# Four gate tiles among block one's first convolution tiles, with buffers of their own for gates and mixer outputs

## Chip, core and metric

The kernel runs on one core of one Trainium2 chip. The metric is the device time of one execution in microseconds. PE is TensorE (PEld its weight loads), DVE VectorE, ACT ScalarE, POOL GpSimd, SP SyncE, which issues the weight DMAs.

## The reference, cut to what matters

Two blocks run one after the other over 256 tokens of width 1024, all in float32. Block one is a Mamba-2 mixer and a gated linear recurrence side by side, and the change lies inside it:

```
hn = rmsnorm(h, norm1_w);  proj = hn @ w_in
gates, z, xbc, dt_raw, lru_x, lru_y = split(proj)
gates = sigmoid(gates + b_branch_gate)
xbc = silu(causal_dwconv(xbc));  dt = softplus(dt_raw + dt_bias)
y = ssd_chunked(xs * dt, dt * a, B, C) + xs * d_skip        # xs, B, C are cut from xbc
y_ssm = rmsnorm_per_group(y * silu(z)) @ w_out_ssm
u = causal_dwconv(lru_x)
r, i = sigmoid(u @ w_r + b_r), sigmoid(u @ w_i + b_i)       # ten heads of 128
log_a = -8 * r * softplus(-lam);  a = exp(log_a)
h_t = a * h_(t-1) + sqrt(1 - a^2) * (i * u)                  # a scan over the tokens
y_lru = (h_t * gelu(lru_y)) @ w_out_lru
h = h + (g_ssm * y_ssm + g_lru * y_lru) @ w_out
```

A feed-forward part follows, and then block two (attention branches and feed-forward, twice), which the change does not touch.

## The kernel before

All weights pass through in 256-column (or 256-row) tiles of 1 MB, in the order of `tile_names()`. For each tile SP loads a raw slot (three of them), ACT copies it to `w_hi` in fp32r, DVE (POOL for a share of later ones) subtracts to get `w_lo`, and PE multiplies: per product the three parts hi*hi, hi*lo, lo*hi, so 16 products or 48 matmuls of 256 columns for a tile. The results stand in PSUM (a ring of four banks, "low", for the tiles; another of four, "high", for small stages).

All engines walk the same list of tiles (`walk`). At tile i each of ACT and DVE does, in this order: `lead(i)`, the split of tile i + 2, which needs PE to have finished tile i - 1; `rest` of tile i - 1; the "mid" stages that `stage_order()` puts at tile i; `evac` of tile i, which needs PE to have finished tile i. PE does the mid stages of a tile halfway through its matmuls (`columns`), and from there its queue is in order: a stage that waits holds the second half of the tile and all that follows.

Tiles of block one before: dt; lx 0 to 4; bc 0 to 3; xs 0, xs 1; then (xs 2+j, ly j, gate j) for j = 0 to 4; xs 7; gate 5 to 7; z and out_ssm tiles. What they cost beside the split:

- `lx`, `bc`, `xs`: ACT opens a convolution (`conv_open`, two instructions), DVE does six steps (`conv`). For bc and xs the rest is a Tanh on ACT and one product on DVE, which ticks `xbc`.
- `gate`: ACT alone, two Tanh of 256 columns. The gates lie over `lru_ab`, the recurrence's a and b, so a gate tile waits for its scans (`lru_scan`).
- `ly`: one Square and one Tanh on ACT, three steps on DVE.

Stages: `gates_ready` (the softplus of dt and lambda: a chain that goes between DVE and ACT, with three ACT table loads), `lru` h (one head: eight short matmuls for two heads, five ACT instructions, two on DVE; it needs the `lam` that gates_ready ends with), `dt_cs` (a cumulative sum on DVE; ACT then issues a DMA that waits for it), `lru_root` (a Sqrt on ACT between two table loads), `lru_scan`, and the SSD: `ssd_open` g (PE: products of B and C and eight transposes of xs), `ssd_decay`, `ssd_val`. `ssd_open` g begins on PE with

```
pe.wait_ge(*at("xbc", 6 + 2 * g))
```

that is for the product of xs tile 2g + 1, since four bc tiles count too. The 21 SSD steps stand one to a tile, in order, from the tile that `places` begins with; the steps with `ssd_open` are steps 0, 5, 10 and 15.

Of the kernel before, what the change touches and what calls it, by code (L numbers as in the profile page):

```python
# [7 lines left out]
F32 = mybir.dt.float32  # L8
# [5 lines left out]
P = 128  # L14
SEQ = 256
# [74 lines left out]

def tile_names():
    names = [("dt", 0)]
    names += [("lx", j) for j in range(5)]
    names += [("bc", j) for j in range(4)]
    names += [("xs", 0), ("xs", 1)]
    for j in range(5):
        names += [("xs", 2 + j), ("ly", j), ("gate", j)]
    names += [("xs", 7)] + [("gate", j) for j in range(5, 8)]
    for g in range(GROUPS):
        names += [("z", 2 * g), ("z", 2 * g + 1)]  # L100
        if g >= 2:
# [85 lines left out]
def stage_order():  # L187
    order = {}

    def put(where, tile, *stages):  # L190
        order.setdefault((where, T[tile]), []).extend(stages)

    put("mid", ("lx", 2), ("gates_ready",))
    for tile, heads in ((("lx", 3), (0, 1)), (("lx", 4), (2, 3))):
        put("mid", tile, *[("lru", h) for h in heads])
    put("mid", ("bc", 0), ("lru", 4), ("lru", 5))
    put("mid", ("bc", 1), ("dt_cs",), ("lru", 6), ("lru", 7))
    put("mid", ("bc", 2), ("lru", 8))
    put("mid", ("bc", 3), ("dt_turn",), ("lru", 9))
    put("mid", ("xs", 0), ("lru_root", 0))  # L200
    put("mid", ("xs", 1), ("lru_root", 1))
    for j in range(5):
        put("mid", ("xs", 2 + j), ("lru_scan", 2 * j), ("lru_scan", 2 * j + 1))

    ssd = []
    for g in range(GROUPS):
# [1 line left out]
        for p in range(4):  # L208
            ssd.append(([("ssd_val", g, p - 1)] if p else []) + [("ssd_decay", g, p)])
    ssd.append([("ssd_val", GROUPS - 1, 3)])  # L210
    places = TILES[T["xs", 3]:T["z", 4] + 1]
    assert len(places) == len(ssd)
    for tile, stages in zip(places, ssd):
        put("mid", tile, *stages)
# [97 lines left out]
def build(nc, w, x_t, x_tok, rows_w, params, consts, consts_2, out_tok):  # L312
    ctx = ExitStack()
    with ctx:
        def sb(name, shape, dt=F32, stack=ctx):
            return stack.enter_context(nc.sbuf_tensor(name, shape, dt))
# [45 lines left out]
        one = ExitStack()  # L362
        xbc = sb("xbc", [P, XBC // P, SEQ], stack=one)
        lru_u = sb("lru_u", [P, LC, SEQ], stack=one)
        lru_ab = sb("lru_ab", [P, 2 * LC, SEQ], stack=one)
        lru_a, lru_b, gates = lru_ab[:, 0:LC, :], lru_ab[:, LC:2 * LC, :], lru_ab[:, 0:2 * DC, :]
        cs_all = sb("cs_all", [P, HPG, SEQ], stack=one)
        xdt = sb("xdt", [P, TT, GC * P], stack=one)
        z_silu = sb("z_silu", [P, 2 * GC, SEQ], stack=one)
# [62 lines left out]
        def pair(x):  # L432
            return x.rearrange("p (k t) -> p k t", k=2)
# [79 lines left out]
        def pe_program():  # L513
# [205 lines left out]
            def rows_ready(name, j):  # L719
                if name == "out_ssm":  # L720
                    pe.wait_ge(*at("y_hi", j + 1))
                    pe.wait_ge(*at("y_lo", j + 1))
                    return 8 + GC * (j // 2 % 2) + 2 * (j % 2)
                if name == "out_lru":
                    pe.wait_ge(*at("lru_hi", j + 1))
                    pe.wait_ge(*at("lru_lo", j + 1))
                    return 2 * j
                if name == "out":
                    pe.wait_ge(*at("mix_hi", j + 1))
                    pe.wait_ge(*at("mix_lo", j + 1))  # L730
                    return 2 * j
                if name in ("ffn_out", "down"):
                    n = j + 1 + (NF1 if name == "down" else 0)
                    pe.wait_ge(*at("h_hi", n))
                    pe.wait_ge(*at("h_lo", n))
                    return 2 * ((j % NF2 if name == "down" else j) % 4)
                l, j = divmod(j, 4)
                if j == 0:
                    pe.wait_ge(*at("ret_hi", 2 * l + 2))
                    pe.wait_ge(*at("ret_lo", 2 * l + 2))  # L740
                else:
                    a = {1: "dsa", 2: "dil0", 3: "dil1"}[j]
                    pe.wait_ge(*at(f"{a}_hi", 2 * l + 2))
                    pe.wait_ge(*at(f"{a}_lo", 2 * l + 2))
                return 2 * j

            def rows(i, name, j):
                count, ring = ROWS[name]
                whole, n = divmod(OUT_ORDER.index(j % 4) + 4 * (j // 4) if name == "out_2" else j, count)
                first, last = n == 0, n == count - 1  # L750
                hi, lo = tile_ready(i)
                k0 = rows_ready(name, j)
                if name not in ("out_ssm", "out_lru"):
                    return token_rows(i, name, j, whole, first, last, ring, hi, lo, k0)
                for b in range(DC // 2):
                    if first:
                        acc[name, b] = take(ring, (name, whole, b), freed_acc(name, whole, b))
                    bank = acc[name, b]
                    for j2 in range(2):
                        for m in range(2):  # L760
                            c0 = (2 * b + m) * P
                            inst = product(bank[:, m * SEQ:(m + 1) * SEQ], hi[:, j2, c0:c0 + P], lo[:, j2, c0:c0 + P],
                                           act_hi[:, k0 + j2, :], act_lo[:, k0 + j2, :], first and j2 == 0 and m == 0,
                                           last and j2 == 1)
                    if last and b < DC // 2 - 1:
                        inst.then_inc(*tick("acc_done"))
                inst.then_inc(*tick("tile_used"))
# [236 lines left out]
        def act_program():  # L1004
# [24 lines left out]
            def evac(i, name, j):  # L1029
# [12 lines left out]
                    k0 = 2 * j + (16 if name == "bc" else 0)  # L1042
                    conv_open(xbc[:, k0:k0 + 2, :], bank, "conv_w", XBC // P, "conv_b", k0, "xbc_open")
                if name == "gate":
                    act.wait_ge(*at("lru_scan", 2 * (j % 5) + 2))
                    act.wait_ge(*at("halved", 3))
                    for m in range(2):
                        inst = fn(gates[:, 2 * j + m, :], bank[:, m * SEQ:(m + 1) * SEQ], ACT.Tanh, scale=0.5,
                                  bias=param("b_gate", 2 * j + m))
                    inst.then_inc(*tick("gate"))  # L1050
# [129 lines left out]

            def norm_split(g):
                for s in range(2):
                    k = 8 + GC * (g % 2) + 2 * s
                    act.wait_ge(*at("gn_x", 2 * g + s + 1))
                    if g >= 2:
                        act.wait_ge(*used("out_ssm", 2 * (g - 2) + s))
                    fn(act_hi[:, k:k + 2, :], pair(tmp[8 + s][:, :]), ACT.Copy).then_inc(*tick("y_hi"))

            def lru_split(n):
                act.wait_ge(*at("lru_out", n + 1))  # L1190
                act.wait_ge(*(used("out_ssm", 4) if n == 4 else used("z", 7)))
                fn(act_hi[:, 2 * n:2 * n + 2, :], lru_u[:, 2 * n:2 * n + 2, :], ACT.Copy).then_inc(*tick("lru_hi"))

            def mix():
                for b in range(4):
# [798 lines left out]
        def pool_program():  # L1994
            def tt(out, a, b, op):
                return nc.gpsimd.tensor_tensor(out, a, b, op)  # L1996

            def low_part(k, n, src):
                return tt(act_lo[:, k:k + n, :], src, act_hi[:, k:k + n, :].bitcast(F32), ALU.subtract)

            split = {"next": 0}

# [22 lines left out]
            def norm_split(g):  # L2025
                for s in range(2):
                    pool.wait_ge(*at("y_hi", 2 * g + s + 1))
                    low_part(8 + GC * (g % 2) + 2 * s, 2, pair(tmp[8 + s][:, :])).then_inc(*tick("y_lo"))

            def lru_split(n):  # L2030
                pool.wait_ge(*at("lru_hi", n + 1))
                low_part(2 * n, 2, lru_u[:, 2 * n:2 * n + 2, :]).then_inc(*tick("lru_lo"))

            pool.wait_ge(*at("x1_hi", 3))
            low_part(4, 2, pair(tmp[8][:, :])).then_inc(*tick("x1_lo_pool"))
# [93 lines left out]
```

## Time and profile before

| | |
|---|---|
| median of 3 runs | 1224.14 us (1223.98 to 1224.82) |
| the profiled execution | 1226.08 us, its span 1224.8 us |
| mean granted clock | 0.993 |
| PE busy | 1185.3 us (97%) |
| DVE busy | 804.1 us (66%) |
| ACT busy | 700.0 us (57%) |
| HBM | 171 GB/s over the span |

An engine's busy time is the union of its instructions. A PE that is busy has work in flight. Of the chain that ended last 79% is PE's. Times below are microseconds from the start of the span.

### The profile page before, as it was taken

The page shows a single profiled execution, that of the slowest core. Times are in us where ns is not written, and L with a number is a line of the kernel's source. Part 1 is how long each engine was busy: PE and PEld are TensorE (multiplying, and loading weights), DVE is VectorE, ACT ScalarE, POOL GpSimd, SP SyncE. Part 2 cuts the span into 40 slices and gives each one's busy share as a digit, 9 for nine tenths or more (in the row PEclk, how much of TensorE's full clock was granted, in tenths as well). Part 3 has the DMA queues.
Part 4 walks back from the last instruction along what each step waited for, and adds up shares of the span by engine and source line. Part 5 has one row for each costly group of instructions (what it writes and reads, how often), then busy time and mean ns, then how long its engine had stood idle before and what let it go on. Part 6 is the DMA issues. An engine that isn't in the chain of part 4 may idle for free.

```text
span 1224.8 us, 18917 instructions
## 1 busy us (share of the span) xinstructions
PE 1185.3 (97%) x7688; PEld 1057.1 (86%) x7688; DVE 804.1 (66%) x1044; ACT 700.0 (57%) x964; POOL 322.6 (26%) x207
## 2 busy tenths in 40 slices
PE   9798999999999999999999899999999989999997
PEld 9798999999998888888999688888899977888886
DVE  7878988677456766675878555555556963555554
ACT  6788766676435443435646856444554396555543
POOL 0000000034931111111475522122225654222211
PEclk9899999999999999999999999999999999999999
DMA  9434756544456665554643346665554433565560
GB/s 291 164 123 154 241 173 202 178 138 142 177 199 238 207 201 176 196 182 139 194 134 122 104 141 207 202 199 181 162 184 147 162 104 104 174 229 185 185 207 34
DMA packets 152437, 210.66 MB, mean 172 GB/s; under 512 B 5504, under 2 KB 132640, under 8 KB 151712
## 3 DMA queue, kind: packets, MB, share of 16 engines
q1 hardware_dynamic: 151584, 205.08, 51.5%
q10 hardware_dynamic: 768, 4.39, 0.9%
q8 instruction: 61, 1.00, 0.3%
q14 instruction: 24, 0.20, 0.0%
HBM read 208.37 MB, written 1.08 MB: 171 GB/s over the span
## 4 chain that ended last, share of the span: by engine, by line
PE 79%; ACT 10%; DVE 8%; issue 2%; DMA 1%; POOL 0%; SPq 0%; ACTq 0%; DVEq 0%
PE banks L534 77%; ACT w_hi L1008 2%; ACT tmp L1008 2%; DVE w_lo L1398 2%; ACT L1008 2%; PE banks L542 1%; DVE xbc L1406 1%; ACT probs_dil L1008 1%; DMA raw<-in_w_in 1%; DVE work L1402 1%; ACT lru_ab L1008 1%; ACT probs_dsa L1008 0%; ACT xbc L1008 0%; DVE lru_u L1406 0%; DVE tmp L1406 0%
## 5 line engine op out<-in xcount | busy, mean ns | idle before, releaser
L534 PE MATMUL banks<-act,w_hi 128*128 128x256 f32 (+1 forms) x3216 | 732.0, 317 | 16.0 <-DVE w_lo L1398 12.0
L534 PEld LDWEIGHTS banks<-act,w_hi 128*128 128x128 f32 x3216 | 524.1, 191 | 65.0 <-issue 19.9
L534 PE MATMUL banks<-act,w_lo 128*128 128x256 f32 (+1 forms) x2040 | 562.2, 282 | 0.0
L1398 DVE TENSOR_TENSOR w_lo<-raw,w_hi 128x2048 fp32r<-128x2048 f32 (+4 forms) x174 | 366.5, 2108 | 222.3 <-ACT w_hi L1008 221.6
L1008 ACT ACTIVATE w_hi<-raw 128x2048 fp32r<-128x2048 f32 (+1 forms) x191 | 359.6, 1884 | 188.6 <-PE banks L534 180.6
L534 PEld LDWEIGHTS banks<-act,w_lo 128*128 128x128 f32 (+1 forms) x2040 | 382.7, 191 | 1.4
L534 PE MATMUL banks<-w_hi,act 128*128 128x512 f32 (+1 forms) x1072 | 323.1, 376 | 7.1 <-DVE act L1398 6.5
L1996 POOL TENSOR_TENSOR w_lo<-raw,w_hi 128x512 fp32r<-128x512 f32 (+1 forms) x146 | 202.6, 1416 | 432.7 <-ACT w_hi L1008 432.7
L534 PEld LDWEIGHTS banks<-w_hi,act 128*128 128x128 f32 x1072 | 197.3, 190 | 46.7 <-issue 11.0
L1996 POOL TENSOR_TENSOR act<-tmp,act 128x512 fp32r<-128x512 f32 x52 | 112.6, 2169 | 451.6 <-ACT act L1008 451.6
L534 PE MATMUL banks<-w_lo,act 128*128 128x512 f32 (+1 forms) x536 | 200.1, 373 | 0.0
L1008 ACT ACTIVATE tmp<-tmp 128x512 f32<-128x512 f32 (+1 forms) x112 | 64.7, 592 | 140.9 <-DVE tmp L1409 140.3
L534 PEld LDWEIGHTS banks<-w_lo,act 128*128 128x128 f32 x536 | 101.8, 190 | 16.1 <-issue 0.5
L1409 DVE TENSOR_REDUCE tmp<-banks 128x512 f32<-128x1024 f32 x54 | 66.0, 1222 | 48.2 <-PE banks L534 48.2
L1008 ACT ACTIVATE act<-tmp 128x512 fp32r<-128x512 f32 x55 | 34.9, 635 | 24.7 <-DVE tmp L1406 22.2
L1008 ACT ACT_TABLE_LOAD x29 | 37.2, 1283 | 1.7 <-PEq L2122 1.2
L1406 DVE SCALAR_TENSOR_TENSOR xbc<-banks,params,xbc 128x255 f32<-128x255 f32 (+2 forms) x72 | 29.1, 474 | 5.9 <-ACT xbc L1008 5.9
L1008 ACT ACTIVATE probs_dil<-probs_dil,small 128x128 f32<-128x128 f32 x64 | 26.2, 451 | 4.8 <-DVE small L1885 2.7
L1008 ACT ACTIVATE tmp<-cs_all,cs_tok 128x256 f32<-128x256 f32 x64 | 23.7, 445 | 0.0
L1406 DVE SCALAR_TENSOR_TENSOR act<-banks,params,act 128x256 fp32r<-128x256 f32 x32 | 13.3, 478 | 15.6 <-ACT act L1008 15.6
L1008 ACT ACTIVATE tmp<-residual 128x512 f32<-128x512 f32 x23 | 14.3, 641 | 9.2 <-DVE residual L1406 9.2
L1398 DVE TENSOR_TENSOR act<-banks,act 128x256 fp32r<-128x256 f32 x12 | 5.0, 419 | 22.1 <-ACT act L1008 21.9
(228 smaller groups left out, 739.7 us busy)
## 6 DMA issues: line engine op xcount, KB each, us to landing
raw<-in_w_in SPq DMA_DIRECT2D x64, 1024.0 KB, 5.3
raw<-in_w_up SPq DMA_DIRECT2D x32, 1024.0 KB, 5.3
raw<-in_w_down SPq DMA_DIRECT2D x32, 1024.0 KB, 5.0
raw<-in_w_ffn_in SPq DMA_DIRECT2D x22, 1024.0 KB, 5.1
raw<-in_w_out SPq DMA_DIRECT2D x12, 1024.0 KB, 5.0
raw<-in_w_ffn_out SPq DMA_DIRECT2D x11, 1024.0 KB, 4.9
raw<-in_w_out_ssm SPq DMA_DIRECT2D x8, 1024.0 KB, 4.9
raw<-in_w_out_lru SPq DMA_DIRECT2D x5, 1024.0 KB, 4.9
```

The lines of the kernel that those rows point to most:

```text
L534: return mm_ops.matmul(out, lhs, rhs, start=start, stop=stop, skip_group_check=True)
L542: return mm_ops.transpose(out, a, c["ident"][0:k, 0:k])
L1008: return ops.activation(out, a, func, bias=bias, scale=scale, accum_out=accum)
L1398: return ops.tensor_tensor(out, a, b, op)
L1402: return ops.tensor_scalar(out, a, s1, None, op0)
L1406: return ops.scalar_tensor_tensor(out=out, in0=a, scalar=s, in1=b, op0=op0, op1=op1, accum_out=accum)
L1409: return ops.tensor_reduce(pair(out[:, :]), both.rearrange("p m (a t) -> p m t a", a=2), AX_X, ALU.add)
L1996: return nc.gpsimd.tensor_tensor(out, a, b, op)
```

## The change

The tiles of block one come in another order: dt; lx 0, 1, 2; gate 0; lx 3; gate 1; lx 4; bc 0; gate 2; bc 1; bc 2; gate 3; bc 3; xs 0, xs 1; then (xs 2+j, gate 4+j, ly j) for j = 0 to 3; xs 6; ly 4; xs 7; then z as before. The softplus (`gates_ready`) goes from lx 2 to gate 0, the ten heads from lx 3 to bc 3 to five tiles from gate 1 to gate 3, `dt_cs` from bc 1 to bc 2, `dt_turn` from bc 3 to xs 0, the scans from the xs tiles to the gate tiles and ly 4. The 21 SSD steps begin at xs 2 and end at z 5, where they began at xs 3 and ended at z 4. The gates get the upper half of `act` (free since the third tile), and the mixer's outputs, which lay there, get `late`, which lies over `lru_ab`; the waits that guarded the old overlays go or are replaced. The bytes, matmuls and vector instructions are the same in number.

```diff
     names = [("dt", 0)]
-    names += [("lx", j) for j in range(5)]
-    names += [("bc", j) for j in range(4)]
-    names += [("xs", 0), ("xs", 1)]
-    for j in range(5):
-        names += [("xs", 2 + j), ("ly", j), ("gate", j)]
-    names += [("xs", 7)] + [("gate", j) for j in range(5, 8)]
+    names += [("lx", 0), ("lx", 1), ("lx", 2), ("gate", 0), ("lx", 3), ("gate", 1), ("lx", 4), ("bc", 0), ("gate", 2), ("bc", 1),
+              ("bc", 2), ("gate", 3), ("bc", 3), ("xs", 0), ("xs", 1)]
+    for j in range(4):
+        names += [("xs", 2 + j), ("gate", 4 + j), ("ly", j)]
+    names += [("xs", 6), ("ly", 4), ("xs", 7)]
...
-    put("mid", ("lx", 2), ("gates_ready",))
-    for tile, heads in ((("lx", 3), (0, 1)), (("lx", 4), (2, 3))):
+    put("mid", ("gate", 0), ("gates_ready",))
+    for tile, heads in ((("gate", 1), (0, 1, 2, 3)), (("bc", 0), (4,)), (("gate", 2), (5, 6, 7)), (("bc", 1), (8,)),
+                        (("gate", 3), (9,))):
         put("mid", tile, *[("lru", h) for h in heads])
-    put("mid", ("bc", 0), ("lru", 4), ("lru", 5))
-    put("mid", ("bc", 1), ("dt_cs",), ("lru", 6), ("lru", 7))
-    put("mid", ("bc", 2), ("lru", 8))
-    put("mid", ("bc", 3), ("dt_turn",), ("lru", 9))
-    put("mid", ("xs", 0), ("lru_root", 0))
+    put("mid", ("bc", 2), ("dt_cs",))
+    put("mid", ("xs", 0), ("dt_turn",), ("lru_root", 0))
     put("mid", ("xs", 1), ("lru_root", 1))
     for j in range(5):
-        put("mid", ("xs", 2 + j), ("lru_scan", 2 * j), ("lru_scan", 2 * j + 1))
+        put("mid", ("gate", 4 + j) if j < 4 else ("ly", 4), ("lru_scan", 2 * j), ("lru_scan", 2 * j + 1))
...
-    places = TILES[T["xs", 3]:T["z", 4] + 1]
+    places = TILES[T["xs", 2]:T["z", 5] + 1]
...
+        with ExitStack() as shared:
+            sb("act_first", [P, 8, 2, SEQ], F32R, stack=shared)
+            gates = sb("gates", [P, 2 * DC, SEQ], stack=shared)
         both_parts = sb("act", [P, 16, 2, SEQ], F32R)
...
-        lru_ab = sb("lru_ab", [P, 2 * LC, SEQ], stack=one)
-        lru_a, lru_b, gates = lru_ab[:, 0:LC, :], lru_ab[:, LC:2 * LC, :], lru_ab[:, 0:2 * DC, :]
+        with ExitStack() as shared:
+            lru_ab = sb("lru_ab", [P, 2 * LC, SEQ], stack=shared)
+        late = sb("late", [P, 2 * LC, SEQ], F32R, stack=one)
...
                 if name == "gate":
-                    act.wait_ge(*at("lru_scan", 2 * (j % 5) + 2))
                     act.wait_ge(*at("halved", 3))
...
             def norm_split(g):
                 for s in range(2):
-                    k = 8 + GC * (g % 2) + 2 * s
+                    k = GC * (g % 2) + 2 * s
+                    act.wait_ge(*at("lru_scan", LC))
...
-                fn(act_hi[:, k:k + 2, :], pair(tmp[8 + s][:, :]), ACT.Copy).then_inc(*tick("y_hi"))
+                fn(y_hi[:, k:k + 2, :], pair(tmp[8 + s][:, :]), ACT.Copy).then_inc(*tick("y_hi"))
...
-                act.wait_ge(*(used("out_ssm", 4) if n == 4 else used("z", 7)))
-                fn(act_hi[:, 2 * n:2 * n + 2, :], lru_u[:, 2 * n:2 * n + 2, :], ACT.Copy).then_inc(*tick("lru_hi"))
+                act.wait_ge(*(at("lru_scan", LC) if n == 4 else used("z", 7)))
+                fn(last_hi if n == 4 else act_hi[:, 2 * n:2 * n + 2, :], lru_u[:, 2 * n:2 * n + 2, :], ACT.Copy).then_inc(*tick("lru_hi"))
```

The same replacement of `act_hi`/`act_lo` by the views of `late` stands in PE's `rows` and in POOL's `low_part`.

## Rows read from the trace of the kernel before

**Rows 1.** Busy time by stretch of time: us, then each engine, granted clock, DMA share.
```profile
33.00:49.70 16.70, 15.45 (x112) 14.65 (x112) 12.78 (x30) 10.66 (x16) 0.00 (x0) 1.00 0.56 179
49.70:55.50 5.80, 0.00 (x0) 0.00 (x0) 5.70 (x14) 5.59 (x11) 0.00 (x0) 0.87 0.00 0
55.50:61.00 5.50, 5.46 (x25) 5.48 (x26) 5.50 (x11) 5.43 (x11) 0.00 (x0) 0.52 0.61 194
61.00:95.00 34.00, 31.81 (x244) 30.64 (x242) 26.40 (x49) 27.38 (x48) 0.00 (x0) 1.00 0.40 126
95.00:122.70 27.70, 23.98 (x193) 23.31 (x193) 23.94 (x41) 23.48 (x26) 0.00 (x0) 1.00 0.50 152
122.70:211.00 88.30, 87.74 (x727) 83.68 (x728) 78.69 (x112) 61.45 (x105) 0.00 (x0) 1.00 0.63 203
211.00:234.00 23.00, 23.00 (x193) 21.64 (x192) 15.05 (x22) 13.47 (x23) 0.00 (x0) 1.00 0.63 212
```

**Rows 2.** Waits of PE from 33 to 130 us: total, times, longest.
```profile
PE banks L534 <- DVE w_lo L1398: 11.8, 7, 5.9
```

**Rows 3.** PE in order of time: start, duration, instruction, count, idle before it.
```profile
55.54 0.77 PE L534 MATMUL banks<-act,w_hi 128*128 128x256 f32 x2 [5.87 <-DVE w_lo L1398]
...
122.66 0.47 PE L534 MATMUL banks<-act,w_hi 128*128 128x256 f32 x2 [1.25 <-DVE w_lo L1398]
...
125.12 0.28 PE L534 MATMUL banks<-act,w_lo 128*128 128x256 f32 x1
...
125.48 0.28 PE L534 MATMUL banks<-act,w_lo 128*128 128x256 f32 x1
125.60 0.82 PE L534 MATMUL banks<-xbc 128*128 128x256 f32 x4
...
152.85 0.88 PE L534 MATMUL banks<-tmp,xdt 128*64 128x256 f32 x8
153.66 0.50 PE L534 MATMUL banks<-act,w_hi 128*128 128x256 f32 x2
```

**Rows 4.** ACT in order of time from softplus to the heads, same columns.
```profile
44.47 0.42 ACT L1008 ACTIVATE cs_all<-cs_all 32x256 f32<-32x256 f32 x1 [2.21 <-DVE small L1398]
...
47.62 1.90 ACT L1008 ACTIVATE w_hi<-raw 128x2048 fp32r<-128x2048 f32 x1
49.53 1.28 ACT L1008 ACT_TABLE_LOAD   x1
...
78.16 0.84 ACT L1008 ACTIVATE tmp<-banks,params 128x256 f32<-128x256 f32 x2 [3.84 <-DVE cs L1591]
...
80.48 0.82 ACT L1008 ACTIVATE tmp<-banks,params 128x256 f32<-128x256 f32 x2
```

**Rows 5.** ACT in order of time around the second root, same columns.
```profile
108.38 1.27 ACT L1008 ACTIVATE lru_ab<-lru_ab 128x1280 f32<-128x1280 f32 x1
109.55 1.00 ACT L1008 ACTIVATE xbc<-banks,params 128x256 f32<-128x256 f32 x2
110.45 1.91 ACT L1008 ACTIVATE w_hi<-raw 128x2048 fp32r<-128x2048 f32 x1
112.38 1.28 ACT L1008 ACT_TABLE_LOAD   x1
113.67 0.63 ACT L1008 ACTIVATE tmp<-xbc 128x512 f32<-128x512 f32 x1
```

**Rows 6.** DVE in order of time: last step of softplus, then tile xs 1.
```profile
50.67 0.17 DVE L1402 TENSOR_SCALAR small<-small 128x10 f32<-128x10 f32 x1
...
110.66 2.43 DVE L1406 SCALAR_TENSOR_TENSOR xbc<-banks,params,xbc 128x255 f32<-128x255 f32 x6 [2.01 <-ACT xbc L1008]
113.00 2.28 DVE L1398 TENSOR_TENSOR w_lo<-raw,w_hi 128x2048 fp32r<-128x2048 f32 x1
115.20 0.68 DVE L1406 SCALAR_TENSOR_TENSOR xbc<-tmp,xbc 128x512 f32<-128x512 f32 x1
```

**Rows 7.** ACT and DVE in order of time after PE has finished tile xs 4.
```profile
150.09 1.02 ACT L1008 ACTIVATE xbc<-banks,params 128x256 f32<-128x256 f32 x2 [1.90 <-PE banks L534]
...
151.72 2.42 DVE L1406 SCALAR_TENSOR_TENSOR xbc<-banks,params,xbc 128x255 f32<-128x255 f32 x6
154.06 2.28 DVE L1398 TENSOR_TENSOR w_lo<-raw,w_hi 128x2048 fp32r<-128x2048 f32 x1
...
156.25 0.68 DVE L1406 SCALAR_TENSOR_TENSOR xbc<-tmp,xbc 128x512 f32<-128x512 f32 x1
```

More of the change, by code:

```diff
@@ L364, in build @@
         lru_u = sb("lru_u", [P, LC, SEQ], stack=one)
-        lru_ab = sb("lru_ab", [P, 2 * LC, SEQ], stack=one)
-        lru_a, lru_b, gates = lru_ab[:, 0:LC, :], lru_ab[:, LC:2 * LC, :], lru_ab[:, 0:2 * DC, :]
+        with ExitStack() as shared:
+            lru_ab = sb("lru_ab", [P, 2 * LC, SEQ], stack=shared)
+        late = sb("late", [P, 2 * LC, SEQ], F32R, stack=one)
+        lru_a, lru_b = lru_ab[:, 0:LC, :], lru_ab[:, LC:2 * LC, :]
+        y_hi, y_lo, last_hi, last_lo = late[:, 0:8, :], late[:, 8:16, :], late[:, 16:18, :], late[:, 18:20, :]
         cs_all = sb("cs_all", [P, HPG, SEQ], stack=one)
@@ L722, in rows_ready @@
                     pe.wait_ge(*at("y_lo", j + 1))
-                    return 8 + GC * (j // 2 % 2) + 2 * (j % 2)
+                    return GC * (j // 2 % 2) + 2 * (j % 2)
                 if name == "out_lru":
@@ L754, in rows @@
                     return token_rows(i, name, j, whole, first, last, ring, hi, lo, k0)
+                x_hi, x_lo = (y_hi, y_lo) if name == "out_ssm" else (act_hi, act_lo)
+                if (name, j) == ("out_lru", 4):
+                    x_hi, x_lo, k0 = last_hi, last_lo, 0
                 for b in range(DC // 2):
@@ L762, in rows @@
                             inst = product(bank[:, m * SEQ:(m + 1) * SEQ], hi[:, j2, c0:c0 + P], lo[:, j2, c0:c0 + P],
-                                           act_hi[:, k0 + j2, :], act_lo[:, k0 + j2, :], first and j2 == 0 and m == 0,
+                                           x_hi[:, k0 + j2, :], x_lo[:, k0 + j2, :], first and j2 == 0 and m == 0,
                                            last and j2 == 1)
@@ L1996, in tt, with low_part @@
                 return nc.gpsimd.tensor_tensor(out, a, b, op)
-            def low_part(k, n, src):
-                return tt(act_lo[:, k:k + n, :], src, act_hi[:, k:k + n, :].bitcast(F32), ALU.subtract)
+            def low_part(k, n, src, hi=act_hi, lo=act_lo):
+                return tt(lo[:, k:k + n, :], src, hi[:, k:k + n, :].bitcast(F32), ALU.subtract)
             split = {"next": 0}
@@ L2027, in norm_split @@
                     pool.wait_ge(*at("y_hi", 2 * g + s + 1))
-                    low_part(8 + GC * (g % 2) + 2 * s, 2, pair(tmp[8 + s][:, :])).then_inc(*tick("y_lo"))
+                    low_part(GC * (g % 2) + 2 * s, 2, pair(tmp[8 + s][:, :]), y_hi, y_lo).then_inc(*tick("y_lo"))
             def lru_split(n):
                 pool.wait_ge(*at("lru_hi", n + 1))
-                low_part(2 * n, 2, lru_u[:, 2 * n:2 * n + 2, :]).then_inc(*tick("lru_lo"))
+                src = lru_u[:, 2 * n:2 * n + 2, :]
+                (low_part(0, 2, src, last_hi, last_lo) if n == 4 else low_part(2 * n, 2, src)).then_inc(*tick("lru_lo"))
             pool.wait_ge(*at("x1_hi", 3))
```

## The prediction, made before the changed kernel was run

> **What bounds the kernel now.** I read the page first: PE is busy in 97% of the span and most of the chain that ended last is PE's, so an edit counts only where it changes PE's idle time or its clock. The busy times by stretch say where that is in block one [rows 1]. PE has nothing in flight from 49.7 to 55.5, its clock is at 0.52 from 55.5 to 61, and it loses 2.2 of 34 us and 3.7 of 27.7 us in the two stretches up to 122.7. From there to 211 it loses 0.6 of 88.3 and then none. The waits name DVE's `w_lo` [rows 2]. It is late because ACT and DVE are full there: softplus and ten heads stand on top of the convolutions. In the stretch 211 to 234, with three of the gate tiles, DVE has 8 of 23 us free. The change carries four gate tiles, which cost DVE only their split, to the place where PE starves.
>
> One tile of PE is 5.76 us: three matmuls (one product) take 0.36, from 125.12 to 125.48 [rows 3], and a tile has 16 products. Without any wait tiles lx 3 to gate 0 (11 tiles, 63.4 us), ten heads (0.86 each, a tile with two heads being 1.72 longer) and 0.5 for `dt_turn` would take 72.5 us. They take from 33.05 to 122.66 [rows 3], so 89.6, and 17.1 us is lost. That is the most the front can give back: 5.87 of it in one gap [rows 3], and 5.5 x (1 - 0.52) = 2.6 by the clock behind it [rows 1].
>
> **Part 1, the front.** I wrote the queues of PE, ACT and DVE side by side, each instruction in program order, beginning when its engine is free and its wait is met. From start to start ACT pays 1.80 for a split, 0.90 for opening a convolution and 0.54 for a Tanh of 512 [rows 5, 7], 2.32 for a head (78.16 to 80.48), 1.30 for a table load [rows 4], 1.17 for a root [rows 5]; DVE 2.34 for a convolution, 2.20 for a split, 0.60 for the product that ticks `xbc` [rows 6]. Done for the kernel before, the table puts xs 3 at 121.7 (trace 122.66) and the losses of 33 to 275 us at 17.6 where the trace has 18.5 (the 17.1 and 1.3 behind it), so it is 0.9 short; I charge the changed kernel with the same 0.9.
>
> For the new order it gives these marks. PE does gate 0 from 33.05 to 39.0, waits 1.9 for lx 3's `w_hi`, and 1.7 for gate 1's `w_lo` (48.2), because DVE has two splits and a convolution to do. Softplus now comes behind gate 1's split on DVE; it ends at 55.2 where it ended at 50.8 [rows 6], and lx 4's split stands behind it, ready at 57.4, just as PE ends gate 1 at 57.6 with four heads in it. So the 5.87 gap is gone, and the clock stays up. Four heads on ACT end at 67.3; behind them stand gate 1's Tanh and gate 2's split, and PE waits 2.4 (69.9 to 72.3). After that it waits only 0.5 at xs 0. The front loses 6.5 in place of 17.1, and PE begins xs 2 at 117.9.
>
> **Part 2, where it goes.** At xs 2 PE meets `ssd_open` 0 halfway, at 120.8, and this waits for the sixth `xbc`: the product of xs 1, the tile just before. In the old order a whole tile lay between (xs 2), and the product, at 115.20 + 0.68 = 115.9 [rows 6], was 9.7 us early for the 125.60 of [rows 3]. So it must be read from ACT when it comes now. From the fourth head's end (67.3) to the second root's end ACT has nine splits (16.2), six heads (13.9), six openings (5.4), five Tanh of 512 (2.7), three gate Tanh (0.71 each, 2.1), two roots (2.3), three table loads (3.9) and the DMA's issue (0.45), 47.0 in all. To this come waits for DVE, of which the table has 9.5: the convolution before each Tanh, and `dt_cs`, where ACT stands still until the sum is there (the 3.84 in [rows 4]). That makes 123.8. Then as in [rows 5, 6]: opening, convolution to 127.2, DVE's split and the product, done at 130.0. PE waits 9.3. The 9.5 is the softest term; the same stretch before has 7.0 (the 3.84 and four of 0.77 to 0.78), and I put its ends at 7 and 12, the wait at 6.8 to 11.8. The front's gain is real, but ACT's and DVE's work ahead of this point has not shrunk, and the wait hands it back.
>
> **Part 3, the same wait twice more.** `ssd_open` 2 is step 10 and now stands at gate 7, right behind xs 5; `ssd_open` 3 is step 15, at z 0, right behind xs 7. `ssd_open` 1 (ly 1) has a tile between and is free. After PE has finished xs 4 (ACT starts at 150.09) the product is there at 156.25 + 0.68 = 156.9 [rows 7], 6.9 later, of which DVE was behind by 0.6. PE arrives half a tile (2.9) and one `ssd_val` (0.8 to 1.0, [rows 3]) later, so 3.8 to 3.9. The difference is 2.4 to 3.1 each; the table has 2.7 and 2.8. Both stand on the path: PE is the bound there [rows 1], and the next splits are ready by 7 us, so nothing else would have held it. Nothing hides them, as the second half of the tile is queued behind.
>
> **Part 4, the clock.** The wait of 9.3 at xs 2 is longer than the 5.87 in which the clock fell. There the half clock cost 2.6 after work had resumed [rows 1]. I take 2.6 again; the ends are 0 (it falls and is back up early) and 5.2 (twice that). The granted clock was 0.52 in the stretch behind that gap, which is the 1.2 GHz level. The Trainium skill says (TensorE: Matmul & The Clock Gate, "What's actually happening") that the throttled state is the default and that activity releases it; by that rule too this change, which looks like one that feeds PE more evenly, pays for a half clock at xs 2. The trace agrees, by that 0.52.
>
> **Part 5, what costs nothing.** The gates' old wait for the scans goes: no engine waited for it, as the scans were done tiles before. `norm_split` gets a wait for the tenth scan, done at ly 4, six tiles before. The fifth LRU split loses its wait for out_ssm 4, but stays queued behind out_ssm 5's stages. The new buffers move no data. The residual's DMA goes two tiles later in SP's queue; the DMA share is 0.4 to 0.6 there [rows 1], its 1 MB and the raw tile behind it have 10 us, and the residual is not read before block one's end. `lru_scan` and `ssd_decay` come closer together at the end: xs 6, ly 4 and xs 7 give DVE about 7.3 each (a split 2.2, a convolution 2.34, the ly steps or scans 2, the SSD's 1.4), against 6.75 for PE, so DVE falls 1.5 behind over three tiles, under the 7 us of lead. Small waits of PE on `ssd_m` and on the norm's total sum to 2.9 in the table, against the 1.3 of before.
>
> **The sum.** After: 1.9 + 1.7 + 2.4 + 0.5 in front, 9.3, 2.7, 2.8, small ones 2.9, clock 2.6, the table's 0.9: 27.7. Before: 18.5. The change costs 9.2 us. Against the profiled execution, 1226.08 of device time, that is 1235.3; it lies 1.9 over the median, so I say 1224.14 + 9.2 = 1233.3. Behind z 5 all is as before and PE-bound, so I see nothing that would take it up.
>
> **Rivals.**
> A, the clock holds or costs little: +6.6, 1230.7. For it: it fell only once in block one. Against: the wait is the longer one.
> B, the other side: the product of xs 1 is ready when PE arrives. If ACT's waits for DVE vanish in the front (9.5 to 0), the product is there at 120.5 and `ssd_open` 0 costs nothing; the sum is then 9.2 - 9.3 - 2.6, that is -2.7, or 1221.4. It decides at 120.8. For it: gates relieve DVE. Against: the convolution must precede its Tanh, and ACT has this pair on its own path each time (the 2.01 of [rows 6] and 3.84 of [rows 4]). With half of that, 4.6 less wait and no clock fall, the sum is +2: within the noise.
> C, DVE goes over its lead behind xs 6 and splits come late, or two falls of the clock: another 3 to 6, 1236 to 1239. For it: 7.3 against 6.75, with steps 13 to 19 beside. Against: PE's own waits at gate 7 and z 0 give DVE time.
> D, table loads cost more than the row shows. A load takes 1.28 (112.38) and the Tanh starts at 113.67 [rows 5], 0.01 later. The Trainium skill (ScalarE: Activation LUTs, "What ACT_TABLE_LOAD costs") gives 2.66 us with a drain. By that page's figure the four loads ahead of the sixth product would add an estimated 4 x 1.38 = 5.5 to the wait, 1239. The row decides against it; its chance lies within C's.
>
> **Chances.** Forecast, 1231.5 to 1235.5: 0.50. A: 0.15. C with D: 0.17. B: 0.08 in full, 0.10 at the half, of which I count most as no change. Faster by over 0.2% (2.4 us, about what a measurement of this kernel can tell from none) 0.09, within it 0.09, slower 0.82. The range leaves out B in full and half of C: 1225 to 1238.
>
> **What would show it.** In the changed trace: no gap near 50 us, clock 1.0 up to 120; PE with about 9 us idle, ended by DVE's `xbc`, at about 121, before `banks<-xbc`; two more of 2 to 3 us near 205 and 243; a low clock only behind the first. Wrong would be: a wait at xs 2 under 5 us, or waits for `w_lo` in the place of those for `xbc`.

## The result, and the profile after

The changed kernel takes 1238.03 us (median of 4 runs, 1237.62 to 1242.12) against 1224.48 for the kernel before (4 runs on the same chip, 1223.98 to 1226.52). The ratio is 1.0114 with a 95% interval of 1.0103 to 1.0126: 13.5 us slower. I had said 1233.3, in a range of 1225 to 1238. The sign and the place were right; the size was 4.7 us short, and the time lies just outside the range.

| | before | changed |
|---|---|---|
| the profiled execution, its span | 1226.08, 1224.8 us | 1237.99, 1236.7 us |
| mean granted clock | 0.993 | 0.989 |
| PE busy | 1185.3 us (97%) | 1188.0 us (96%) |
| DVE, ACT busy | 804.1, 700.0 us | 806.3, 700.2 us |
| tile z 6 begins on PE | 287.29 | 300.84 |

All of it is lost ahead of z 6, 13.55 us by the last line. (The two spans differ by 11.9, because the profiled execution of before lost 1.6 more in one wait at 1008 us, which the change doesn't touch.)

Waits of PE from 33 to 300 us in the changed kernel: what it waited for, then us in total, times, longest. Line 537 is the matmul helper, 534 in the kernel before.

```profile
PE banks L537 <- DVE xbc L1412: 14.5, 3, 8.6
PE banks L537 <- DVE tmp L1404: 3.8, 4, 3.0
PE banks L537 <- DVE w_lo L1404: 3.8, 2, 2.3
PE banks L537 <- ACT w_hi L1014: 1.8, 1, 1.8
```

Of the 11.8 for `w_lo` of [rows 2] 3.8 is left, and the gap of 5.87 of [rows 3] is gone. Three waits for `xbc`, none of which was there before, cost 14.5. That is what I had described. What I hadn't is in the second line: 3.8 for `tmp`, of which 2.97 is one wait for the norm at z 5. Here are PE's instructions at which three of the four long waits end, start and duration first, the idle time ahead and its releaser last:

```profile
131.00 1.41 PE L537 MATMUL banks<-xbc 128*128 128x256 f32 x3 [8.60 <-DVE xbc L1412]
...
205.83 0.88 PE L537 MATMUL banks<-xbc 128*128 128x256 f32 x2 [2.87 <-DVE xbc L1412]
...
283.32 1.13 PE L537 MATMUL banks<-tmp,mean_group 128*128 128x256 f32 x4 [2.97 <-DVE tmp L1404]
```

The fourth is 3.06 at z 0 (242.10 to 245.15). Busy time by stretch, as in [rows 1] (length, PE, PEld, DVE, ACT, POOL, granted clock, DMA share, GB/s):

```profile
33.00:48.20 15.20, 11.93 (x97) 11.58 (x97) 12.87 (x24) 8.18 (x10) 0.00 (x0) 1.00 0.71 239
70.00:76.50 6.50, 4.17 (x23) 3.99 (x22) 6.30 (x8) 6.43 (x12) 0.00 (x0) 0.74 0.40 126
76.50:122.40 45.90, 45.90 (x366) 45.00 (x365) 35.77 (x59) 35.87 (x53) 0.00 (x0) 1.00 0.53 167
122.40:131.00 8.60, 0.01 (x1) 0.03 (x1) 6.44 (x10) 6.82 (x7) 0.00 (x0) 0.81 0.62 196
131.00:134.50 3.50, 3.50 (x14) 3.32 (x15) 1.38 (x3) 0.00 (x0) 0.00 (x0) 0.50 1.00 365
202.90:210.00 7.10, 4.23 (x22) 4.08 (x21) 6.86 (x10) 0.63 (x1) 0.00 (x0) 0.76 0.62 200
237.00:250.00 13.00, 9.95 (x84) 9.42 (x84) 10.12 (x18) 4.51 (x8) 0.00 (x0) 1.00 0.73 243
280.00:289.00 9.00, 6.03 (x37) 5.68 (x34) 5.36 (x6) 7.29 (x10) 6.17 (x4) 0.81 0.12 40
```

The third line is the front's gain: 45.9 us in which PE doesn't stop once, where before it lost something in nearly every tile. The clock column tells the rest. It is low behind four gaps, of 2.33, 8.6, 2.87 and 2.97 us, and stays at 1.00 behind the one of 3.06 (seventh line). In the fifth line it is 0.50, the 1.2 GHz level, over 3.5 us of work: 1.75 us lost. Elsewhere it is (1 - 0.74) x 6.5 = 1.7, (1 - 0.76) x 7.1 = 1.7 and (1 - 0.81) x 9.0 = 1.7, each with the low stretch wholly in work. Together 6.9 us, against the 2.6 of [rows 1] before.

### The profile page after: what moved, and what is told of

The parts are those of the page before. It is cut to its first block, busy times and chain, and to the rows that moved or that the text cites. A ratio compares the mean times of both kernels' runs of the same rounds, so it can differ in the third digit from the quotient of the medians.

```text
span 1236.7 us, 18911 instructions
## 1 busy us (share of the span) xinstructions
PE 1188.0 (96%) x7688; PEld 1060.0 (86%) x7688; DVE 806.3 (65%) x1044; ACT 700.2 (57%) x964; POOL 322.9 (26%) x207
## 4 chain that ended last, share of the span: by engine, by line
PE 74%; DVE 12%; ACT 10%; issue 3%; DMA 1%; POOL 0%; SPq 0%; ACTq 0%; DVEq 0%
PE banks L537 72%; ACT w_hi L1014 2%; DVE xbc L1412 2%; DVE w_lo L1404 2%; ACT tmp L1014 2%; PE banks L545 2%; ACT L1014 1%; ACT probs_dil L1014 1%; DVE lru_u L1412 1%; DMA raw<-in_w_in 1%; DVE tmp L1404 1%; DVE work L1408 1%; ACT xbc L1014 1%; DVE tmp L1412 0%; ACT probs_dsa L1014 0%
## 5 line engine op out<-in xcount | busy, mean ns | idle before, releaser
L537 PE MATMUL banks<-act,w_hi 128*128 128x256 f32 (+1 forms) x2928 | 680.5, 320 | 10.4 <-DVE w_lo L1404 4.0
L537 PEld LDWEIGHTS banks<-act,w_hi 128*128 128x128 f32 x2928 | 480.4, 191 | 58.7 <-issue 13.1
L537 PE MATMUL banks<-act,w_lo 128*128 128x256 f32 x1896 | 522.0, 282 | 0.0
L537 PEld LDWEIGHTS banks<-act,w_lo 128*128 128x128 f32 x1896 | 355.7, 191 | 1.4
L2002 POOL TENSOR_TENSOR act<-tmp,act 128x512 fp32r<-128x512 f32 x44 | 102.4, 2327 | 440.1 <-ACT act L1014 440.1
L537 PE MATMUL banks<-late,w_hi 128*128 128x256 f32 x288 | 52.2, 284 | 0.0
L537 PEld LDWEIGHTS banks<-late,w_hi 128*128 128x128 f32 x288 | 45.0, 192 | 0.1
L537 PE MATMUL banks<-late,w_lo 128*128 128x256 f32 x144 | 40.7, 283 | 0.0
L1014 ACT ACTIVATE act<-tmp 128x512 fp32r<-128x512 f32 x47 | 29.9, 635 | 4.6 <-DVE tmp L1412 2.1
L537 PEld LDWEIGHTS banks<-late,w_lo 128*128 128x128 f32 x144 | 27.6, 192 | 0.0
```

The source lines that it names most:

```text
L537: return mm_ops.matmul(out, lhs, rhs, start=start, stop=stop, skip_group_check=True)
L1014: return ops.activation(out, a, func, bias=bias, scale=scale, accum_out=accum)
```

## The experiments

Two theories stood after the result. Mine: three `ssd_open` stand a tile too close behind the `xs` tile whose product they read; these waits, the norm's and the clock behind them are the whole loss. The rival: something else that comes with the change, the buffers or the new neighbours on ACT and DVE, has moved the loss, and `xbc` is only where it shows. Each run is timed beside the kernel before, whose median stands with it where it matters. The traces and pages quoted are of one profiled execution each.

One number of the prediction has to be set right first. It says that in the old order a whole tile lay between xs 1 and `ssd_open` 0. By the list of tiles it was three: xs 2, ly 0 and gate 0, as the stage stood in the middle of xs 3. `ssd_open` 2 and 3 had three and two tiles between them and the xs tile that they read. The change put each of the three stages straight behind it, with none between.

### The three openings one tile later

```diff
+    for g in (0, 2, 3):
+        ssd[5 * g].remove(("ssd_open", g))
+        ssd[5 * g + 1].insert(0, ("ssd_open", g))
```

> The changed kernel with ssd_open 0, 2 and 3 each one tile later (gate 4, ly 3, z 1), so that a whole tile lies between an xs tile and the stage that reads it. Theory (PE waits for the product of the xs tile just before it): the waits of 8.6, 2.9 and 3.1 us go, and with them the clock falls at 127.7 and 206.2 that cost about 1.7 each; 1238.0 - 14.6 - 3.4 gives 1220.0, between 1218 and 1222, faster than the kernel before. Rival (the front has gained nothing, DVE and ACT are behind anyway, and PE then waits for w_lo or the SSD's masks instead): 1228 or more, with new waits of 5 us or more between 120 and 260.

Measured: 1225.12 (1222.72 to 1226.10), ratio 0.9996 (0.9987 to 1.0006). One tile more, for three openings of one stage, gives back 13 us, and the changed kernel stands where the kernel before does. Its waits of PE from 33 to 300:

```profile
PE banks L540 <- DVE xbc L1415: 2.9, 1, 2.9
...
PE banks L540 <- DVE tmp L1407: 3.8, 4, 3.0
```

```profile
130.67 1.22 PE L540 MATMUL banks<-xbc 128*128 128x256 f32 x3 [2.87 <-DVE xbc L1415]
```

The waits at `ssd_open` 2 and 3 are gone. That at `ssd_open` 0 isn't: PE reaches it at 127.80, a tile later, and the product of xs 1 still ends at 130.5. I had expected no wait here. The time lies 5 us over the forecast, of which this wait and the low clock behind it (130.9 to 134.3) are 4.6, and the reason is on view: the product comes no earlier, and a tile's 5.8 us isn't enough for a lag of 8.6. One tile between is less than the three of the kernel before. The norm's 2.98 is untouched.

### The first opening alone

The same edit with `for g in (0,)`.

> Only ssd_open 0 one tile later (gate 4). Theory: 8.6 of wait and 1.7 of half clock go: 1227.7, the waits at gate 7 and z 0 stay at 2.9 and 3.1. Rival (PE, ahead again, finds the later products later by as much): the waits at gate 7 and z 0 grow by some us each, 1231 to 1235.

Measured: 1233.31 (1230.96 to 1235.54), ratio 1.0068 (1.0050 to 1.0086). That is 4.7 of the change's loss. Waits at the three openings are now 3.85, 2.87 and 3.05 and at the norm 2.97. So the 8.6 shrank to 3.85 by 4.75, and the later two stayed as they were: each is its own wait, not an echo of the first. Against the run above, openings 2 and 3 are worth another 8.2: their waits sum to 5.9, and the 2.3 left are put down to the clock, which was low behind both of them here (1.7 and 2.9 us lost in the profiled execution, the slowest of the four) and behind neither there. (The wait at opening 0 is 1.0 shorter there because PE came 0.9 later, its clock having fallen at 73; it ends at the same time, 130.7, in both.) In this kernel's profile the clock was low behind each of the four waits, for 3.4 us behind the first two and 6.8 us behind the last two.

### The buffers alone

The kernel before, with its own order of tiles and stages, and the new buffers (`gates` in `act_first`, mixer outputs in `late`, with their waits).

```diff
-        lru_ab = sb("lru_ab", [P, 2 * LC, SEQ], stack=one)
+        with ExitStack() as shared:
+            lru_ab = sb("lru_ab", [P, 2 * LC, SEQ], stack=shared)
+        late = sb("late", [P, 2 * LC, SEQ], F32R, stack=one)
...
-                    act.wait_ge(*at("lru_scan", 2 * (j % 5) + 2))
```

> The order of tiles and stages of the kernel before, with the changed kernel's buffers and waits only. Theory (buffers cost and give nothing): within 1 us of the kernel before, 1224.5. Rival (the new buffers are part of the loss, by reads of late on PE or by the wait for the tenth scan): 1227 or more.

Measured: 1225.10 (1223.96 to 1225.91), ratio 1.0002 (0.9992 to 1.0011), with the waits of before:

```profile
PE banks L540 <- DVE w_lo L1407: 11.9, 7, 5.9
```

The rival loses its first half: places and waits of the buffers cost nothing.

### The kernel before with an early opening

```diff
+    ssd[0].remove(("ssd_open", 0))
+    put("mid", ("xs", 2), ("ssd_open", 0))
```

> The kernel before with ssd_open 0 alone one xs tile earlier, at xs 2, straight behind xs 1. Theory: PE arrives at 104.4 and waits for the product at 115.9, so 11.5 us; the waits for w_lo of 0.7, 1.3 and 1.3 behind it go, ly 1 starts 7.7 later than at 130.0, and a clock fall adds 1.7 to 2.6: 1224.5 + 9.4 to 10.3, so 1234 to 1235. Rival (the wait only takes the place of waits that PE has anyway, since ACT and DVE are the bound there): 1224 to 1227.

Measured: 1234.39 (1232.86 to 1235.38), ratio 1.0074 (1.0058 to 1.0091).

```profile
115.40 1.41 PE L536 MATMUL banks<-xbc 128*128 128x256 f32 x3 [11.43 <-DVE xbc L1408]
```

A stage moved from the middle of xs 3 to the middle of xs 2, three tiles earlier in the old order, costs 9.6 us between the medians, 9.1 by the ratio: the wait of 11.43, plus 2.6 for a half clock that lasts 5.2 us into the work behind it, less 3.2, three of the four waits for `w_lo` from 101 to 123 (among those of [rows 2]), which vanish while PE stands. That is 10.8; the stretch after it (tile ly 1) begins 9.6 us later than before in an execution that had begun 0.6 earlier, so 10.2. So taking the tiles away between a product and its reader is enough for such a loss, without any gate tile.

### The norm's wait

At z 4 DVE does `norm_split` 0 ahead of the last two mask products, which become a stage of their own.

```diff
-    put("mid", ("z", 4), ("norm_split", 0), ("norm_sum", 1))
+    put("mid", ("z", 4), ("norm_split", 0), ("last_mask",), ("norm_sum", 1))
```

> The changed kernel with one thing turned round on DVE at z 4: the first group's norm (reciprocal and two scalings) stands ahead of the last two mask products, which z 4 did not have in the old order. Theory (those products, 2.6 us beside POOL's split, push the norm's total late): PE's wait for the mean at z 5 falls from 2.97 to under 1.2, and with it the clock fall at 284.7 (1.7): 1238.0 - 1.9 - 1.7, so 1234.4, between 1233 and 1236.5. Rival (the wait comes from the outputs' new buffer): no change, 1237 to 1239.

Measured: 1234.92 (1233.48 to 1238.76), ratio 1.0086 (1.0070 to 1.0103). DVE's instructions there from the split on, of the changed kernel and then of this one (a convolution step of 0.48 is left out behind each split):

```profile
272.47 1.23 DVE L1404 TENSOR_TENSOR w_lo<-raw,w_hi 128x1024 fp32r<-128x1024 f32 x1 [0.32 <-ACT w_hi L1014]
...
274.27 2.57 DVE L1404 TENSOR_TENSOR tmp<-tmp,cb_mask 128x384 f32<-128x384 f32 x2
276.76 1.74 DVE L1653 RECIPROCAL rstd<-rstd 128x256 f32<-128x256 f32 x1
278.53 1.67 DVE L1412 SCALAR_TENSOR_TENSOR tmp<-z_silu,params,rstd 128x256 f32<-128x256 f32 x4
```

```profile
275.81 1.22 DVE L1404 TENSOR_TENSOR w_lo<-raw,w_hi 128x1024 fp32r<-128x1024 f32 x1 [0.31 <-ACT w_hi L1014]
...
277.39 1.75 DVE L1655 RECIPROCAL rstd<-rstd 128x256 f32<-128x256 f32 x1
279.17 1.74 DVE L1412 SCALAR_TENSOR_TENSOR tmp<-z_silu,params,rstd 128x256 f32<-128x256 f32 x4
280.83 1.01 DVE L1404 TENSOR_TENSOR tmp<-tmp,cb_mask 128x384 f32<-128x384 f32 x2
```

```profile
PE banks L537 <- DVE tmp L1404: 0.8, 3, 0.3
```

In the changed kernel the mask products hold the reciprocal back by 2.5. Done later they take 1.01, and the norm's wait of 2.97 is no longer among PE's waits. That is worth 3.1 us between the medians; I had expected 3.6. The profiled execution is the slowest of the four (1238.76): the clock didn't fall behind the norm, but it did at z 0, and was low for 6.8 us there. Of the 3.1 us, how much is the wait and how much the clock isn't shown.

### PE kept at work through the waits

34 products of a constant with itself (`mm`, two matmul records each) ahead of the wait of `ssd_open` 0 and 10 ahead of those of 2 and 3, into a bank that the stage then begins anew. They add no work to another engine and are to end before the wait does; only the clock should differ.

```diff
+                for _ in range({0: 34, 2: 10, 3: 10}.get(g, 0)):
+                    mm(bank[:, 0:P], c["mean_d"], c["mean_d"])
```

> The changed kernel with matmuls on a constant put in front of the three waits for xbc (34, 10 and 10 calls, 7.7, 2.3 and 2.3 us of PE at full clock), into the bank that the stage then overwrites. The waits themselves stay. Theory (half clock behind the waits costs 1.7 at xs 2 and 1.6 at gate 7): these two falls go and the time is 1238.0 - 3.3, so 1234.7, between 1233.5 and 1236. Rival (the clock costs nothing on the path): 1238 or more.

Measured: 1236.17 (1234.62 to 1236.46), ratio 1.0087 (1.0072 to 1.0103). 1.9 gained where I expected 3.3. The 34 calls were too few: PE still stood 1.91 at xs 2, and the clock fell there and behind the norm; behind gate 7's it didn't. So it was done again with 39, 12 and 12, and 12 ahead of the norm's mean:

> The changed kernel with all four long waits of PE filled by matmuls on a constant: 39 calls ahead of the wait at xs 2 (8.8 us), 12 each at gate 7, z 0 and ahead of the norm's mean at z 5 (2.7 us each). The waits stay. Theory (the term of the sum that was too small is the clock, three falls of 1.6 to 1.7 us behind these waits): no half clock between 100 and 400 us, and 1238.0 - 5 + 0.5 for the calls' ends gives 1233.5, between 1232 and 1235. Rival (the falls take nothing from the path): 1237 or more.

Measured: 1233.89 (1233.18 to 1234.41), ratio 1.0071 (1.0057 to 1.0085). One stretch, 100 to 300 us:

```profile
100.00:300.00 200.00, 197.00 (x1625) 188.40 (x1624) 158.99 (x223) 138.54 (x209) 13.12 (x9) 1.00 0.50 164
```

The same stretch of the changed kernel has a clock of 0.97. Here it is 1.00, the profile has no low clock ahead of 689 us, and z 6 begins at 296.36 and not at 300.84. The wait at xs 2 ends at 131.33, no earlier than in the changed kernel (this execution began 0.4 later), though PE came to it 1.0 earlier by the same start: the low clock at 73 had been taken up by that wait. So of the 13.5 us the clock has about 4, by 1238.03 - 1233.89, and some 9 that remain are waits. Between the two profiled executions, from the same start, z 6 comes 4.9 earlier.

### Both mended

Later openings with the norm's order on DVE:

> Both repairs on the changed kernel: ssd_open 0, 2 and 3 one tile later, and the first norm ahead of the last mask products on DVE. Theory: 2 to 3.5 us under the kernel with the later opens alone (1225.1): 1221.6 to 1223.1, faster than the kernel before by 0.1 to 0.25%. Rival (what is won falls to other waits): 1225.

Measured: 1221.46 (1220.01 to 1223.46) against 1224.91, ratio 0.9971 (0.9959 to 0.9982). Then ACT's DMA for `cs`, which waits for DVE's sum, goes from bc 2 to bc 3:

```diff
+    put("mid", ("bc", 3), ("cs_spill",))
```

> The same, and ACT issues the DMA of the cumulative sums one tile later (bc 3 in place of bc 2), so that it does not stand 3.8 us for DVE. Theory (ACT's queue up to the second root sets when the sixth xbc product comes): the product comes 2 to 3.8 us earlier, PE's remaining wait of 2.9 at gate 4 goes to under 1 and its clock fall with it: 1218.5 to 1221.5. Rival (DVE, not ACT, sets it): the product stays at about 130.6 and the time at that of the kernel without this.

Measured: 1220.73 (1218.34 to 1221.39), ratio 0.9960 (0.9948 to 0.9973). This is the fastest of all: the change of order is worth 0.4% once its readers stand a tile further from their products and the norm goes first on DVE. The last edit gave less than I expected of it:

```profile
PE banks L541 <- DVE xbc L1416: 2.7, 1, 2.7
```

The product that PE waits for is read 2.5 earlier (128.31 in place of 130.79, of which 0.8 is an earlier start of the whole execution), and the wait stays at 2.7 because PE, too, arrives earlier: in this profile its clock didn't fall at 73, nor at 42. Between the last two medians the intervals overlap; the DMA's place is not shown to matter.

### The first opening still later

The kernel just described, with `ssd_open` 0 and the masks that read it behind gate 4's matmuls instead of in its middle.

> The best kernel so far (later opens, norm ahead, the sums' DMA later; 1220.7) with ssd_open 0 and the first decay behind gate 4's matmuls in place of between them. Theory: PE comes there 2.9 us later, its last wait for xbc of 2.7 us and the fall behind it go, less up to 2 of wait for the first masks at ly 0: 1217 to 1219.5. Rival (the masks come so much later that PE waits for them instead): 1220.5 to 1222.

Measured: 1220.67 (1220.35 to 1221.35), ratio 0.9964 (0.9952 to 0.9977): no change, as the rival had it.

```profile
PE banks L544 <- DVE tmp L1411: 4.6, 4, 3.8
```

The wait for `xbc` is gone, and one of 3.76 for the first masks stands in its place, ahead of `ssd_val`. The chain from the sixth product over the masks to the values has its own length, and PE met it here at the next reader.

### The softplus back at its old place

The changed kernel, with `gates_ready` at lx 2.

```diff
-    put("mid", ("gate", 0), ("gates_ready",))
+    put("mid", ("lx", 2), ("gates_ready",))
```

> The changed kernel with softplus back at lx 2, ahead of the splits of gate 1 and lx 4 on both queues. Theory (what the front wins the wait at xs 2 takes back, since ACT's and DVE's queues set when the sixth xbc product comes): PE waits some 7 us more before gate 1 (w_lo at about 55.4 in place of 48.0), and 6 to 8 us less at xs 2 (8.6 to 1 or 2), so the time stays at 1238 within 2 us. Rival (the front's waits and the wait at xs 2 add up): 1243 to 1246.

Measured: 1244.57 (1241.34 to 1246.08), ratio 1.0153 (1.0134 to 1.0171). The time is the rival's; its reason is only a part of it.

```profile
PE banks L537 <- DVE xbc L1412: 12.9, 3, 7.0
PE banks L537 <- DVE w_lo L1404: 7.2, 1, 7.2
```

With softplus early DVE brings gate 1's split late, and PE stands 7.2 there (48.36 to 55.54). My theory was that this is taken from the 8.6 at xs 2, as the sixth product's time was set by ACT and DVE alone. But ACT's first head needs PE's matmuls, which stand in gate 1 behind the same wait:

```profile
61.25 0.84 ACT L1014 ACTIVATE tmp<-banks,params 128x256 f32<-128x256 f32 x2 [5.08 <-PE banks L537]
```

So ACT loses 5.08 as well, the product comes at 133.9 in place of 130.9, and the wait at xs 2 falls only from 8.6 to 7.0. PE's waits for `w_lo` and `xbc` together are yet only 1.8 longer than in the changed kernel (7.2 and 12.9 against 3.8 and 14.5). Most of the rest is the clock. In the profiled execution it was low for longer behind the waits at z 0 and of the norm, here with their stretches:

```profile
247.00:254.00 7.00, 5.62 (x24) 5.47 (x25) 3.57 (x6) 0.00 (x0) 0.00 (x0) 0.51 0.49 160
288.00:295.00 7.00, 5.85 (x23) 5.48 (x24) 4.99 (x5) 5.07 (x5) 4.21 (x3) 0.51 0.08 6
```

That is 2.8 and 2.9 us lost in work, where the changed kernel lost nothing and 1.7; behind the three openings and the norm it sums to 9.3 against 5.2. With the 3.1 by which the wait at xs 2 ends later this makes 7.2, and z 6 begins 7.0 later. It is the change's move of softplus that spares the front the gap of 7.2.

## Why the prediction came out as it did

**Part 1, the front: right in its waits, wrong in its clock.** Forecast 6.5 of waits; measured 1.83 for lx 3's `w_hi`, 1.44 and 2.33 for `w_lo`, none at xs 0: 5.6. PE began xs 2 at 119.37 where I had 117.9. The waits were 0.9 shorter than forecast, and PE still came 1.5 later. 1.7 of these 2.4 are the low clock from 73.0 to 76.5, behind the 2.33 us gap, in a place where I had written "the clock stays up"; the other 0.7 are of the size of the 0.9 that I had added for what the table misses.

**Part 2, the wait at xs 2: right.** Forecast 9.3, measured 8.59. The prediction's "a whole tile lay between" for the old order was wrong, as said above (three tiles did), but nothing in the sum was worked out from it. ACT's second root ended at 124.6 (I had 123.8), with 9.6 of waits for DVE ahead of it (9.5):

```profile
ACT tmp L1014 <- DVE xbc L1412: 5.8, 4, 2.3
ACT xbc L1014 <- DVE cs L1597: 3.8, 1, 3.8
```

and the product came at the end of what I had written down: convolution, split, product.

```profile
125.62 2.43 DVE L1412 SCALAR_TENSOR_TENSOR xbc<-banks,params,xbc 128x255 f32<-128x255 f32 x6 [2.01 <-ACT xbc L1014]
127.97 2.28 DVE L1404 TENSOR_TENSOR w_lo<-raw,w_hi 128x2048 fp32r<-128x2048 f32 x1
130.17 0.69 DVE L1412 SCALAR_TENSOR_TENSOR xbc<-tmp,xbc 128x512 f32<-128x512 f32 x1
```

Its end is 130.86; forecast 130.0. One sentence behind it doesn't hold in general: I took the pace of ACT and DVE up to the sixth product as theirs alone. Where a wait of PE holds a head back it isn't, as the run with the early softplus shows.

**Part 3, the two later waits: right.** 2.87 and 3.06 for 2.7 and 2.8. The run of the first opening alone shows that they stand by themselves.

**Part 4, the clock: the term that failed.** Forecast 2.6, one fall, with ends 0 to 5.2. Measured in the profiled execution: four falls of 1.7 each. The one at 73 is free, since the wait at xs 2 takes it up; the other three, 5.2 in sum, are on the path. The term at xs 2 itself was too large (1.75). What I left out is the clock behind gaps under 3 us. The working took it as a matter of the longest gap only, "the clock fell once", and [rows 3] holds just one gap over 2 us in block one, so nothing in those rows said that 2.7 is safe. The same trace had the answer further on, in the part that the change doesn't touch: PE stands 3.01 us there from 678.0 to 681.0, and the clock is low from 682.0 to 685.4:

```profile
680.00:684.00 4.00, 3.00 (x9) 2.48 (x10) 3.13 (x9) 3.97 (x9) 2.00 (x2) 0.75 0.16 37
```

So "it fell only once in block one" was true and no ground for charging one fall. The kept-busy run prices the clock at 4.1 us between medians. That is less than 5.2. The mean granted clock was 0.984 to 0.989 in the changed kernel's four executions and 0.993 to 0.996 in the kept-busy ones, so the profiled execution of the latter, at 0.996, was among those that lost least to it. Where the clock fell in the others isn't known; only one trace of each kernel is kept.

**Part 5, the small waits: too small by 1.8.** Forecast 2.9 for the `ssd_m` waits and the norm, measured 0.88, 0.25, 0.34, 0.26 and 2.97, so 4.7. For the norm my table had 0.7, which the prediction doesn't give by itself. It moved the last decay to z 4 with its durations of before: two mask products at about 1.0. They took 2.57, beside POOL's share of the split, and stood ahead of the reciprocal on the norm's path. In the kernel before they were done a tile earlier, and the reciprocal came right behind the split at z 4 (DVE's instructions there; a convolution step of 0.48 lies between split and reciprocal):

```profile
257.96 1.02 DVE L1398 TENSOR_TENSOR tmp<-tmp,cb_mask 128x384 f32<-128x384 f32 x2
...
263.06 1.23 DVE L1398 TENSOR_TENSOR w_lo<-raw,w_hi 128x1024 fp32r<-128x1024 f32 x1 [0.32 <-ACT w_hi L1008]
...
264.64 1.74 DVE L1647 RECIPROCAL rstd<-rstd 128x256 f32<-128x256 f32 x1
```

The move had been told in this part ("the 21 steps end at z 5"), but only its amount of work was charged, not who is queued behind it. The rest of part 5 held: buffers and gates' waits cost nothing by their own run, and none of PE's waits is for the residual or for a split behind xs 6.

**The sum.** From the forecast 9.2: +0.9 as the wait at xs 2 ended at 131.0 and not at 120.8 + 9.3, -0.9 for the clock behind it, +0.4 for the two later waits and +1.7 for the clock behind the first, +1.8 for the small ones and +1.7 for the clock behind the norm. That makes 14.8, where z 6 came 13.55 later. Of the 1.25 over, up to 0.9 can be the term that I had added for what the table misses; the rest isn't placed. So the step that failed is the clock's term: 2.6 for one fall behind the longest wait, where the runs show three falls on the path, 5.2 us, behind waits of 8.6, 2.9 and 3.0. The small waits' term is the second, 2.9 for 4.7.

**The rivals.** C ("two falls of the clock", 1236 to 1239) is what came, with more falls than two and without DVE going over its lead; I gave it 0.17. A (the clock holds) can be read off the kept-busy run: 1233.9 in place of my 1230.7, and the 3.2 between fit the waits that were mis-sized: 0.9 at xs 2, 0.4 at the two later openings and 1.8 for the small ones. B did not come: the product isn't ready, as ACT still had 9.6 of waits for DVE. D is out: the table loads ahead of the sixth product fit into 124.6 at their old durations. Had I charged 1.7 behind each of the two later waits, which I had at 2.7 and 2.8, the forecast would have been 1236.7; the profiled execution had a fall behind only one of them.

## What to carry to other kernels

When tiles change order, list for each stage with a wait how many tiles lie between it and the producer of what it reads, and compare this with how far the producing engines are behind PE at that point: going from three tiles between to none cost 8.6 us at the first opening here, and one tile between gave back 13 us over the three. A relief in front did not shorten the queues of the engines that were the bound here; the wait moved to the next reader. And price the clock behind each new gap by itself, not behind the longest only; in the changed kernel the half clock took 1.7 of PE's time behind each of four gaps from 2.3 to 8.6 us. Last, when a step of one engine moves to another tile, look at who is queued behind it there: 2.5 us of masks ahead of the norm cost 3.1.

## What the runs showed of the hardware

The clock's fall doesn't follow a gap's length alone. In the changed kernel it was at the 1.2 GHz level behind gaps of 2.33, 2.87 and 2.97 us and not behind 3.06; with the first opening later it fell behind 3.05, and in the kept-busy profile a gap of 2.34 at 71 us left it at 1.00, where the changed kernel's at the same place did not. Nor is 1.7 us the most. In the run with the norm first the clock was low for 6.8 us behind the same wait of 3.06 at z 0, which costs 2.8:

```profile
244.60:251.50 6.90, 5.69 (x25) 5.54 (x26) 3.40 (x6) 0.00 (x0) 0.00 (x0) 0.51 0.50 160
```

And with the early softplus it fell at 42.3, behind a gap of 1.83 that ends at 40.9, the longest since 12 us, where the changed kernel's same gap left it at 1.00. So a wait of 2 to 3 us was that wait plus nothing, 1.7 or up to 2.9 us, and no run tells ahead which.

Two mask products on DVE, each of 384 columns and two inputs in SBUF, took 2.57 in the changed kernel and 1.01 in the run with the norm first. In the one each began while an instruction of POOL's was running, those of this first row:

```profile
272.52 3.90 POOL L2002 TENSOR_TENSOR w_lo<-raw,w_hi 128x512 fp32r<-128x512 f32 x2 [246.81 <-ACT w_hi L1014]
280.22 2.49 POOL L2002 TENSOR_TENSOR late<-tmp,late 128x512 fp32r<-128x512 f32 x2 [3.80 <-ACT late L1014]
```

In the other they began at 280.83, just ahead of POOL's pair for `late`, and it was this pair that took longer, 3.77 for 2.49 (its second instruction beside the next product on DVE, begun at 282.72):

```profile
280.92 3.77 POOL L2004 TENSOR_TENSOR late<-tmp,late 128x512 fp32r<-128x512 f32 x2 [1.49 <-ACT late L1014]
```

Either way some 1.3 to 1.6 us goes to the one that came second. The Trainium skill names the contention (SBUF — State Buffer, "Who interferes with whom"): a DVE instruction with two inputs in SBUF contends with a GpSimd instruction that reads SBUF. These rows agree. In the kernel before, POOL has nothing to do when the two mask products run (257.96, shown above; its first instruction there is at 263.11), and they take 1.02.
